# Two-layer hybrid trunk on eight cores: sigmoid, SiLU and the reciprocal square roots of the RWKV stage written with exp and ln

## The reference

```python
for l in range(2):
    h = rmsnorm(x, g_pre) * (1 + scale) + shift
    u_a, z_a, shifted, gate_a, gate_b = split(h @ w_in)
    y_a = pooled_mixer(u_a) * pool_scale * silu(z_a)
    xs = token_shift(shifted, mu_shift)
    r, k, v, z_b, w_lo, a_lo = split(xs)
    w_log = -softplus(-(w0 + tanh(w_lo) @ w_decay_up)) - 0.5
    decay = exp(-exp(w_log))            # = exp(-exp(-0.5) * sigmoid(w0 + ...))
    a = sigmoid(a0 + a_lo @ w_aaa_up)
    if l == 1:
        v = v + (v_first - v) * sigmoid(mv0 + mv @ w_mv_up)
    kk = k * k_k; kk = kk / max(norm(kk), 1e-12)       # per head
    k = k * (1 + (a - 1) * k_a)
    o = wkv7(r, decay, k, v, -kk, kk * a)              # delta-rule recurrence
    o = (o - mean(o)) * rsqrt(var(o) + 64e-5) * lnx_g + lnx_b
    y_b = (o + bonus) * silu(z_b)
    out = (sigmoid(gate_a) * (y_a @ w_br_a) + sigmoid(gate_b) * (y_b @ w_br_b)) @ w_out
    x = x + gate * rmsnorm(out, g_post)
```

## Time and profile before

| | |
|---|---|
| median of 3 runs | 11694.79 us (11688.37 to 11706.34) |
| profiled execution, its own time | 11688.7 us |
| its span on the slowest core (core 3) | 11687.2 us; the cores lie between 11645.5 and 11687.2 |
| busy: PE / DVE / ACT | 7005 / 5053 / 2890 us |
| granted clock, mean of the span | 0.646 |
| ACT_TABLE_LOAD | 638, 818.6 us in all |
| reciprocals of 128 x 256 or less (VectorE) | 264, 450.4 us in all |

### The profile page before, as it was taken

How to read it: one execution, slowest core, us unless ns; L and a number is a source line. 1 busy time by engine, 2 the same in 40 slices (tenths; PEclk the granted TensorE clock), 3 DMA queues, 4 the chain that set the end, 5 groups by cost and what they waited for, 6 DMA issues and landing times.

```text
span 11687.2 us, 132920 instructions; the slowest of 8 cores (11645.5 to 11687.2 us)
## 1 busy us (share of the span) xinstructions
PE 7005.0 (60%) x46208; PEld 3941.2 (34%) x46208; DVE 5053.3 (43%) x10247; ACT 2890.2 (25%) x5171; POOL 238.7 (2%) x327
## 2 busy tenths in 40 slices
PE   3899924555455454547738999245554554545577
PEld 1344413333333333333313444133333333333333
DVE  1000065555555555554310000665556566565543
ACT  1201103333333333320121011133333333333201
POOL 1000000000000000000010000000000000000000
PEclk6899955555555555558958999555555555555589
DMA  7455320000000000003474443200000000000033
GB/s 132 106 113 103 69 74 14 12 12 12 14 12 12 13 11 14 12 19 89 131 140 100 115 102 69 77 14 12 12 12 14 12 13 14 10 15 12 20 92 128
DMA packets 379992, 571.82 MB, mean 49 GB/s; under 512 B 35468, under 2 KB 299660, under 8 KB 362436
## 3 DMA queue, kind: packets, MB, share of 16 engines
q0 software_dynamic: 165120, 170.61, 10.3%
q1 hardware_dynamic: 214216, 392.71, 10.1%
HBM read 555.52 MB, written 178.27 MB: 63 GB/s over the span
## 4 chain that ended last, share of the span: by engine, by line
PE 40%; DVE 25%; issue 13%; ACT 11%; DMA 8%; another core or an unknown queue 1%; DVEq 1%; POOL 0%; ACTq 0%; SPq 0%; POOLq 0%
PE pb L317 38%; DVE arenaB L334 8%; DVE arenaA L334 6%; ACT L330 4%; ACT arenaA L330 3%; ACT arenaB L330 3%; PE pT L321 2%; DVE arenaB L351 2%; DVE arenaA L354 2%; DMA arenaB<-w_ada 2%; DVE arenaA L344 1%; DVE Hb L344 1%; DMA projT<-arenaA 1%; DVE arenaB L344 1%
## 5 line engine op out<-in xcount | busy, mean ns | idle before, releaser
L317 PE MATMUL pb<-arenaB 64*64 64x64 bf16 (+3 forms) x27008 | 2868.5, 244 | 2426.1 <-DVE arenaB L334 2136.2
L317 PEld LDWEIGHTS pb<-arenaB 64*64 64x64 bf16 (+3 forms) x27008 | 2011.8, 138 | 3290.8 <-issue 2782.0
L317 PE MATMUL pb<-big,arenaB 128*128 128x512 bf16 x12480 | 2723.4, 381 | 183.7 <-DMA arenaB<-w_br_a 122.6
L317 PEld LDWEIGHTS pb<-big,arenaB 128*128 128x128 bf16 x12480 | 1222.2, 98 | 1684.0 <-issue 238.0
L330 ACT ACTIVATE arenaB<-pb 64x512 bf16<-64x512 f32 (+2 forms) x1344 | 716.6, 565 | 2693.1 <-PE pb L317 1922.9
L330 ACT ACT_TABLE_LOAD x638 | 818.6, 1283 | 1788.6 <-PE pb L317 989.3
L330 ACT ACTIVATE arenaA<-pb 128x64 f32<-128x64 f32 (+4 forms) x1252 | 523.8, 419 | 2606.6 <-PE pb L317 2287.5
L334 DVE TENSOR_TENSOR arenaA<-arenaA 128x256 f32<-128x256 f32 (+3 forms) x1822 | 842.6, 478 | 179.8 <-DMA arenaA<-projT 50.6
L321 PE MATMUL pT<-ident,arenaB 128*64 128x128 bf16 x2048 | 503.9, 308 | 398.3 <-DVE arenaB L351 185.7
L351 DVE COPY arenaA<-pb 128x512 f32<-128x512 f32 (+1 forms) x168 | 116.1, 691 | 1300.0 <-PE pb L317 1009.7
L351 DVE CAST arenaB<-pb 64x512 bf16<-64x512 f32 (+1 forms) x768 | 481.4, 628 | 343.1 <-PE pb L317 343.1
(11 more groups left out here) (88 smaller groups left out, 4001.7 us busy)
## 6 DMA issues: line engine op xcount, KB each, us to landing
projT<-arenaA SPq DMA_DIRECT2D x392, 256.0 KB, 2.5
arenaB<-w_in POOLq DMA_DIRECT2D x160, 512.0 KB, 12.9
arenaA<-projT SPq DMA_DIRECT2D x448, 128.5 KB, 2.9
arenaB<-w_ada POOLq DMA_DIRECT2D x96, 512.0 KB, 13.9
sgT<-arenaA SPq DMA_DIRECT2D x256, 128.0 KB, 1.9
arenaA<-projT SPq DMA_DIRECT2D x32, 1024.0 KB, 7.2
arenaB<-sgT SPq DMA_DIRECT2D x64, 512.0 KB, 3.8
arenaA<-x SPq DMA_DIRECT2D x16, 1024.0 KB, 5.0
```

What stands on the lines that cost most here:

```text
L317: self.P.op("pe", lambda e: e.matmul(out, lhsT, rhs, start=start, stop=stop), r, w, cost=max(64.0, self._n(out)) / 2400.0 + 0.01)
```

## The change

In the RWKV stage each Sigmoid becomes three activations: Exp(-x - b), Ln(1 + that), Exp(-that); the bias is the negated column from a new tile `negc`, the 1 comes from a new tile `onec`. The norm of kk becomes max(sum, 1e-24), Ln, Exp(-0.5 times), without Sqrt and reciprocal; the max moves ahead of the activation and reads PSUM. LayerNorm's Sqrt and reciprocal become Ln and Exp(-0.5 times). Silu(z) becomes z, multiplied in by one more VectorE operation, times a sigmoid made the same way. Activations of the other stages (Tanh, the Silu and Sigmoid of the projection, the Sqrt of the outer norms) stay.

```diff
+    negc = k.sb("negc", [128, 24], F32)
+    onec = k.sb("onec", [128, 1], F32)
...
+    k.memset(onec, 1.0, ["onec"])
...
+        k.ts1(negc, cols[l][:, CW0:CW0 + 24], -1.0, ALU.mult, [ck], ["negc"])
...
-                kk_.act(f_g, X1[:, 0:W], AF.Sigmoid, [K1, ck], ["f_Sp"], bias=col(l, CMV0 + p))
+                kk_.act(f_g, X1[:, 0:W], AF.Exp, [K1, "negc"], ["f_Sp"], bias=negc[:, 16 + p:17 + p], scale=-1.0)
+                kk_.act(f_g, f_g, AF.Ln, ["f_Sp", "onec"], ["f_Sp"], bias=onec)
+                kk_.act(f_g, f_g, AF.Exp, ["f_Sp"], ["f_Sp"], scale=-1.0)
...
-            kk_.act(f_sg, X0[:, 0:W], AF.Sigmoid, [K0, ck], ["f_sg"], bias=col(l, CW0 + p))
-            kk_.act(f_a, X0[:, W:2 * W], AF.Sigmoid, [K0, ck], ["f_a"], bias=col(l, CA0 + p))
+            kk_.act(f_sg, X0[:, 0:W], AF.Exp, [K0, "negc"], ["f_sg"], bias=negc[:, p:p + 1], scale=-1.0)
+            kk_.act(f_a, X0[:, W:2 * W], AF.Exp, [K0, "negc"], ["f_a"], bias=negc[:, 8 + p:9 + p], scale=-1.0)
+            kk_.act(f_sg, f_sg, AF.Ln, ["f_sg", "onec"], ["f_sg"], bias=onec)
+            kk_.act(f_a, f_a, AF.Ln, ["f_a", "onec"], ["f_a"], bias=onec)
+            kk_.act(f_sg, f_sg, AF.Exp, ["f_sg"], ["f_sg"], scale=-1.0)
+            kk_.act(f_a, f_a, AF.Exp, ["f_a"], ["f_a"], scale=-1.0)
...
-            kk_.act(f_t1, X1[:, 0:W], AF.Sqrt, [K1], ["f_t1"])
-            kk_.ts1(f_t1, f_t1, 1e-12, ALU.max, ["f_t1"], ["f_t1"])
-            kk_.recip(f_t1, f_t1, ["f_t1"], ["f_t1"])
+            kk_.ts1(f_t1, X1[:, 0:W], 1e-24, ALU.max, [K1], ["f_t1"])
+            kk_.act(f_t1, f_t1, AF.Ln, ["f_t1"], ["f_t1"])
+            kk_.act(f_t1, f_t1, AF.Exp, ["f_t1"], ["f_t1"], scale=-0.5)
...
-            kk_.act(f_t1, X0[:, W:2 * W], AF.Sqrt, [K0, "epsl"], ["f_t1"], bias=epsl)
-            kk_.recip(f_t1, f_t1, ["f_t1"], ["f_t1"])
+            kk_.act(f_t1, X0[:, W:2 * W], AF.Ln, [K0, "epsl"], ["f_t1"], bias=epsl)
+            kk_.act(f_t1, f_t1, AF.Exp, ["f_t1"], ["f_t1"], scale=-0.5)
...
-            kk_.act(f_t1, f_z, AF.Silu, ["f_z"], ["f_t1"])
+            kk_.act(f_t1, f_z, AF.Exp, ["f_z"], ["f_t1"], scale=-1.0)
+            kk_.act(f_t1, f_t1, AF.Ln, ["f_t1", "onec"], ["f_t1"], bias=onec)
+            kk_.act(f_t1, f_t1, AF.Exp, ["f_t1"], ["f_t1"], scale=-1.0)
+            kk_.tt(f_d, f_d, f_z, ALU.mult, ["f_d", "f_z"], ["f_d"])
             kk_.tt(ybT[:, p, t0:t0 + W], f_d, f_t1, ALU.mult, ["f_d", "f_t1"], ["ybT%d" % p])
```

## The result

The changed kernel takes 10887 us (median of 9 runs, 10857 to 11146) against 11711 (median of 10). The ratio is 0.9303, 95% interval 0.9272 to 0.9334: 817 us less. I had forecast 400 less, 11,295, so the direction was right and the size half of what came. The profiled execution has a span of 10862.1 us.

A forecast was written before the change was run, and what follows sets the result against it. Each stream's own dependency chain plus in-order queue waits was taken as the bound; savings of 7.0 and 5.9 us times 32 gave 415 us, the other count 350; 395 taken, 11,295 us, range 11,120 to 11,600.

The forecast's parts named there:

- The second way of counting: Gain from chain-of-waits shares: loads 440 us plus reciprocals 227, less 55% of the added ScalarE work, giving 350 us.
- a): Sigmoids and norm of kk: 6.76 us before, 3.9 after, new max covered by VectorE's idle time; saving 2.9 us.
- b): Decay exponentials: the table load ahead of them goes, saving 1.28 us.
- c): LayerNorm, from the load to the multiply: 3.73 us before, 1.18 after; saving 2.55 us.
- d): Silu: load and Silu 1.71 us before, Exp, Ln, Exp 1.49 after, added multiply covered; 0.3 us taken as saved.
- e): Layer 1's value gate: its Sigmoid of 0.47 us becomes Exp, Ln, Exp at 1.55 us; cost 1.1 us.
- f): One-off negc and onec: two tiny VectorE instructions under the stage's loading, costing nothing.
- Order alone is worth some 70 us a layer: Planner's interleaving, either sign; reason given: layer 1 has 64 us more chain, yet the stages are equally long.
- 1 (no shared table): Exp and Ln don't share a loaded table, so RWKV-stage loads rise to 8 and 10 an iteration: 12,012 us; chance 0.13.
- 2 (given back): ScalarE's six chained activations delay the other stream's evictions; the chain holds nearly all new work: 11,600 us; chance 0.20.
- 3 (more than forecast): Whole gross gain of 667 us, with the new work off the chain: 11,020 us; chance 0.07.
- The drain of 1.38 us a switch: Extra cost at each ScalarE table switch: 440 us more off, to about 10,850; chance 0.01.

The follow-up runs named there:

- the run without loads: Kernel before, queue order untouched, with Sigmoid, Sqrt and Silu of the RWKV stage replaced one for one by Exp: 11359 us, ratio 0.9625.

## Why the prediction was wrong

**The step that failed** is the first: "The bound is each stream's own dependency chain, plus the places where the in-order queues make it wait for the other stream", from which the sum took one stream's savings "times 32". In the settled order of the kernel before there is no own chain. Each engine takes the operations of both streams in one written order, one cycle of waits runs through both, and an operation on it counts once per pair, whichever stream it belongs to: all four reciprocals of a pair counted (5.6 us), and taking two of them out of one stream sped up both. Layer 0's account of a period, forecast and measured:

| term | forecast | measured |
|---|---|---|
| loads | 5 x 1.28 = -6.4 | -10.3 |
| reciprocals, with a gap each | -3.7 | -5.7 (a 0.29 us multiplication left in place) |
| all new work | +3.1, the remainder | +2.7 |
| new order | 0 | -0.6 |
| sum | -7.0 | -13.9 |

In layer 1 it is -5.9 forecast and -12.3 measured (loads -8.6, reciprocals -5.6, new work +2.3, order -0.4). The order's term is small against what a median of wandering periods can tell. That 13.9 is twice 7.0 is luck: counting each term for both streams would give 12.8, 7.4 and 6.2 us, and only the first two come near what was measured. The new work of both streams cost less than I had set for one; apart from the sigmoids' share, no run shows why.

**The second way of counting** (667 us gross, 350 net) failed for a related reason: I took the shares by line. They hold a reciprocal whole only where its result was awaited. Where another stream's instruction stood behind it, its time is in "issue" (1.61 us twice a period). Measured against 3.8 us a period by the shares, the reciprocals were worth 5.7, and the loads 10.3 against 7.4.

**Rows and steps.** ScalarE's timeline of the changed kernel, the six activations of the sigmoids and then Ln and Exp of the norm:

```profile
3084.35 1.02 ACT L330 ACTIVATE arenaA<-pb,negc 128x256 f32<-128x256 f32 x2
3085.27 0.90 ACT L330 ACTIVATE arenaA<-arenaA,onec 128x256 f32<-128x256 f32 x2
3086.07 0.71 ACT L330 ACTIVATE arenaA<-arenaA 128x256 f32<-128x256 f32 x2
...
3088.61 0.92 ACT L330 ACTIVATE arenaA<-arenaA 128x256 f32<-128x256 f32 x2 [0.82 <-DVE arenaA L337]
```

a) The six take 2.43 us (forecast 2.45), but the cover for the new max was missing: ScalarE waits 0.82 us for it here (L337). Over layer 0's 64 iterations 2.4 us lie between the six and the norm's Ln in the median, and from the first Exp to the end of the norm's Exp it takes 6.2 us, where 3.9 was forecast (6.8 before, from the load to the reciprocal's end). So the 2.9 us of this place did not come at this place. b) counted 1.28 us for the decay exponentials' load; the chain held 0.46 of each, as VectorE worked on beside it. c) holds, to 0.02 us. d) counted Silu's load as relief of 1.28; of the pair's two one was not on the chain. e) The value gate's 1.1 us is not to be seen: all new work costs 2.3 us in layer 1 and 2.7 in layer 0. f) Nothing, as forecast: all but the two stages takes 4568 us before and 4567 after. The estimate that all new work would cost 55 to 100% of its 577 us was too dear: 2.7 and 2.3 us a pair, 32 times each, are 160 us, 28%. "Order alone is worth some 70 us a layer" holds: the new order gives 0.2% on the new operations and 0.9%, 109 us for both layers, on the old. Its reason was misread: the stages are not equally long, layer 1's takes 16 us more.

**Rivals.** 1 (no shared table) is out by the 10 loads. 2 (given back) is out: the new work gave back 160 us. 3 (more than forecast), given 0.07, is what happened, and its price of 11,020 was still not low enough. Of its reasons, "The relief on ScalarE and VectorE also counts for the other stream" is the right one and should have been worked out instead of being named beside the sum; "the new work off the chain" is not, as 28% of it counted. The drain of 1.38 us a switch, which the Trainium skill's page "ScalarE: Activation LUTs", section "What ACT_TABLE_LOAD costs", adds, would also have given a larger saving. The trace disagrees, with 0.02 us between the eviction's end and the load, and the run without loads saved 10.3 and 8.6 us a period, less than both streams' 12.8 us of loads alone.

## What to carry to other kernels

Where several streams share in-order queues in a fixed order, read one whole period of the chain of waits piece by piece, and count an operation wherever the chain passes over its time, also as "issue" right behind its start: in layer 0 that reading gives 10.0 and 5.8 us for measured 10.3 and 5.7, where the shares by line gave 7.4 and 3.8; in layer 1 it gives 10.7 for 8.6 and 5.8 for 5.6. Don't price added work the same way: 577 us of it cost 160, and the sigmoids, which stand ahead of the rest of an iteration, carried some six tenths. And look at how far the streams run apart before the operations: here, a limit of 8 operations on their lead was worth 5%.

## What the runs showed of the hardware

An Ln with a bias column takes 0.50 us on 128 x 256 from SBUF, the Exp without one 0.41 to 0.42. Ten table loads serve the whole program, so an Exp behind an Ln needs none. ScalarE's Ln and Exp (0.47 and 0.42) replace a table load, a Sqrt and a VectorE reciprocal (1.28, 0.47 and 1.75).
